# Root-mean-square roots on four columns of 128 tokens, spread over the rows by TensorE, in a two-layer trunk on one Trainium2 core

## The reference

```python
def rmsnorm(x, g, eps=1e-6):
    xf = x.astype(F32)
    y = xf * lax.rsqrt(jnp.mean(xf * xf, axis=-1, keepdims=True) + eps)
    return (y * g.astype(F32)).astype(x.dtype)

for i in range(DEPTH):
    h = rmsnorm(x, norm_mix[i])
    x = x + (even_mixer if i % 2 == 0 else mlstm_mixer)(h, ...)
    x = x + peer(rmsnorm(x, norm_ffn[i]), ...)
    gate = sigmoid(rmsnorm(x, norm_ple[i]) @ ple_gate[i])
    x = x + gate * (p[i] @ ple_w[i])
return rmsnorm(x, norm_final)
```

## Time and profile before

| | before |
|---|---|
| median of 3 runs | 4248.63 us (4247.73 to 4251.1) |
| the profiled execution | 4250.18 us, span 4248.7 us, mean granted clock 0.994 |
| TensorE busy | 4185.4 us, 99% |
| VectorE, ScalarE, POOL busy | 2731.2 us (64%), 2064.9 us (49%), 1319.8 us (31%) |
| chain that ended last | PE 83%, DVE 6%, ACT 5%, issue 4%, POOL 1% |

### The profile page before, as it was taken

One profiled execution on the slowest core, in us unless ns is written; L12 is line 12 of the kernel. 1 busy time (PEld: TensorE's weight loads), 2 busy tenths in 40 slices (PEclk: granted clock), 3 DMA queues, 4 the chain that ended last, 5 costly groups with the idle time before them and its releaser, 6 DMA issues.

```text
span 4248.7 us, 61062 instructions
## 1 busy us (share of the span) xinstructions
PE 4185.4 (99%) x19171; PEld 3421.3 (81%) x19171; DVE 2731.2 (64%) x5672; ACT 2064.9 (49%) x4042; POOL 1319.8 (31%) x1648
## 2 busy tenths in 40 slices
PE   8998999999999999999999999999999999999998
PEld 6666888888888888888788888888888888888886
DVE  3647898777764444444777765997778744444445
ACT  3756333877763333333555553335777833333334
POOL 0311446877750000001200002457778710000001
PEclk9999999999999999999999999999999999999999
DMA  3112334555566565652222223335555575655542
GB/s 116 60 58 77 110 117 158 206 188 186 184 248 233 173 217 173 205 185 99 84 86 84 89 84 105 111 134 195 185 205 181 203 275 176 214 176 202 188 138 85
DMA packets 181372, 657.75 MB, mean 155 GB/s; under 512 B 17664, under 2 KB 17792, under 8 KB 176352
## 3 DMA queue, kind: packets, MB, share of 16 engines
q1 hardware_dynamic: 102960, 371.41, 25.7%
q0 software_dynamic: 41392, 217.39, 14.5%
q10 hardware_dynamic: 36864, 67.13, 4.3%
HBM read 511.09 MB, written 144.77 MB: 154 GB/s over the span
## 4 chain that ended last, share of the span: by engine, by line
PE 83%; DVE 6%; ACT 5%; issue 4%; POOL 1%; ACTq 0%; DVEq 0%; POOLq 0%
PE ps L185 76%; PE ps L1564 2%; ACT first_scaled L1583 2%; ACT w_hi L158 1%; DVE od_tmp L371 1%; POOL w_lo L171 1%; DVE w_lo L164 1%; PE ps L1147 1%; PE ps L874 1%; PE ps L1837 1%; ACT gelu L1074 0%; PE ps L2063 0%; PE ps L522 0%; PE ps L523 0%; DVE gate_group L1493 0%
## 5 line engine op out<-in xcount | busy, mean ns | idle before, releaser
L164 DVE TENSOR_TENSOR w_lo<-w_raw,w_hi 128x1024 fp32r<-128x1024 f32 x585 | 719.4, 1230 | 1050.2 <-ACT w_hi L158 1046.4
L158 ACT ACTIVATE w_hi<-w_raw 128x1024 fp32r<-128x1024 f32 x694 | 734.6, 1058 | 1096.9 <-PE ps L185 961.1
L185 PE MATMUL ps<-h_hi,w_hi 128*128 128x512 f32 x3080 | 1214.4, 394 | 20.6 <-DVE h_lo L314 10.7
L185 PE MATMUL ps<-h_hi,w_lo 128*128 128x512 f32 x3080 | 1201.2, 390 | 0.0
L185 PE MATMUL ps<-h_lo,w_hi 128*128 128x512 f32 x3080 | 1200.5, 390 | 0.0
L185 PE MATMUL ps<-y_hi,w_hi 128*128 128x512 f32 x2368 | 926.6, 391 | 2.4 <-POOL w_lo L171 1.7
L185 PE MATMUL ps<-y_hi,w_lo 128*128 128x512 f32 x2368 | 923.3, 390 | 0.0
L185 PE MATMUL ps<-y_lo,w_hi 128*128 128x512 f32 x2368 | 923.0, 390 | 0.0
L1545 POOL TENSOR_SCALAR second_hot<-iota,token_keys 128x128 fp32r<-128x128 f32 x1024 | 724.9, 722 | 0.0
L185 PEld LDWEIGHTS ps<-h_hi,w_hi 128*128 128x128 f32 x3080 | 579.2, 188 | 152.1 <-issue 22.5
L185 PEld LDWEIGHTS ps<-h_hi,w_lo 128*128 128x128 f32 x3080 | 578.9, 188 | 122.6
(11 more groups left out here) (347 smaller groups left out, 3529.3 us busy)
## 6 DMA issues: line engine op xcount, KB each, us to landing
w_raw<-in_u SPq DMA_DIRECT2D x256, 512.0 KB, 3.3
w_raw<-in_v SPq DMA_DIRECT2D x256, 512.0 KB, 3.3
gates<-gate_group POOLq DMA_DIRECT2D x36, 2048.0 KB, 7.9
acts<-gelu ACTq DMA_DIRECT2D x256, 256.0 KB, 2.1
gate_block<-gates POOLq DMA_DIRECT2D x32, 2048.0 KB, 18.0
gelu_block<-acts POOLq DMA_DIRECT2D x30, 2048.0 KB, 11.5
w_raw<-in_od_in SPq DMA_DIRECT2D x65, 512.0 KB, 3.3
w_raw<-in_ev_in SPq DMA_DIRECT2D x33, 512.0 KB, 3.3
```

What stands on the lines that cost most here:

```text
L158: self.nc.scalar.activation(self.wh[:, slot % SPL, :], self.raw[:, slot, :], ACT.Copy).then_inc(self.sig("w_hi_ready").sem, 1)
L164: self.nc.vector.tensor_tensor(self.wl[:, slot % SPL, :], self.raw[:, slot, :], self.wh[:, slot % SPL, :].bitcast(F32), ALU.subtract).then ...
L185: ins = self.nc.tensor.matmul(out, a[:, s, w], b[:, k, :], start=first and j == 0 and m == 0, stop=last and j == n - 1 and m == 2)
```

## The change

A new class `Root` makes all eight roots. The sum over partitions is turned round: the squares are the weights, 128 tokens at a time, and one column of ones moves. Four such matmuls leave four columns, 128 tokens in the partitions of each. ScalarE and VectorE work on these 128x4. TensorE spreads them back over the rows: the column, broadcast to 128 columns, is the weights, and the identity moves. ScalarE copies the spread rows to SBUF (`act_keep`), except for the final norm, whose scalings read PSUM.

```diff
+class Root:
+    def pe_sums(self, pe, squares, part=0):
+        p = self.p
+        for j in range(TT):
+            c = part * TT + j
+            ins = p.nc.tensor.matmul(p.ps[:, self.bank, c:c + 1], squares[:, j * P:(j + 1) * P], p.ones[:, 0:1],
+                                     start=True, stop=True, skip_group_check=True)
+        return ins
+    def dve_parts(self, dve):
+        p = self.p
+        p.nc.vector.tensor_reduce(p.root[:, :], p.ps[:, self.bank, 0:TT * self.parts].rearrange(
+            "p (k j) -> p j k", j=TT), AX_X, ALU.add).then_inc(self.added.sem, 1)
+    def act_make(self, act):
+        a, p = self.p.nc.scalar, self.p
+        src = p.ps[:, self.bank, 0:TT]
+        if self.parts > 1:
+            act.wait_ge(self.added.sem, self.added.at(1))
+            src = p.root[:, :]
+        a.activation(p.root[:, :], src, ACT.Copy, scale=1.0 / (DK * P), bias=EPS).then_inc(self.made.sem, 1)
+        act.wait_ge(self.made.sem, self.made.at(1))
+        a.activation(p.root[:, :], p.root[:, :], ACT.Sqrt).then_inc(self.made.sem, 1)
+    def dve_invert(self, dve):
+        dve.wait_ge(self.made.sem, self.made.at(2))
+        self.p.nc.vector.reciprocal(self.p.root[:, :], self.p.root[:, :]).then_inc(self.inverted.sem, 1)
+    def pe_spread(self, pe):
+        p = self.p
+        pe.wait_ge(self.inverted.sem, self.inverted.at(1))
+        for j in range(TT):
+            ins = p.nc.tensor.matmul(p.ps[:, self.bank, j * P:(j + 1) * P], p.root[:, j:j + 1].to_broadcast([P, P]),
+                                     p.ident[:, :], start=True, stop=True, skip_group_check=True)
+        ins.then_inc(self.spread.sem, 1)
+    def pe_product(self, pe, u, out, rh, rl):
+        def tile(k):
+            if k == 3:
+                self.pe_spread(pe)
+        p = self.p
+        p.product(pe, u, u % RAW, out, rh, rl, wait_tile=tile).then_inc(p.sig("w_used").sem, 1)
+    def act_keep(self, act, rstd):
+        act.wait_ge(self.spread.sem, self.spread.at(1))
+        self.p.nc.scalar.activation(rstd, self.p.ps[:, self.bank, :], ACT.Copy).then_inc(self.kept.sem, 1)
```

`parts` is 8 in the front (a set of four columns for each tile), 2 in the final norm, 1 elsewhere. `Norm` calls these in place of L307, L309, L320, L326 and L341; the one-column table load stays. The spread is placed inside the next unit, ahead of its tile 3, by `pe_product`:

```diff
 EvenFront, TensorE
+            if n == 1:
+                self.norm.root.pe_product(pe, u0 + 1, p.ps[:, self.EARLY_BANK[1], :], p.hh, p.hl)
+                continue
 EvenFront, ScalarE
         for n in range(1, len(EARLY)):
             ahead(n)
+            if n == 1:
+                self.norm.root.act_keep(act, self.norm.rstd)
 EvenSSD, TensorE
-        t.matmul(p.ps[:, 3, :], p.ones[:, :], self.total, start=True, stop=True).then_inc(self.ss.sem, 1)
+        self.root.pe_sums(pe, self.total).then_inc(self.ss.sem, 1)
         pe.wait_ge(self.zl.sem, self.zl.at(DK))
-        for k in range(DK, 2 * DK):
+        pe.wait_ge(self.ov.sem, self.ov.at(DK - 1))
+        self.root.pe_product(pe, u0 + DK, p.ps[:, 6, :], p.hh, p.hl)
+        for k in range(DK + 1, 2 * DK):
 EvenSSD, VectorE
-        dve.wait_ge(self.root.sem, self.root.at(2))
+        self.root.dve_invert(dve)
         ahead(DK)
-        v.reciprocal(self.rstd, self.rstd).then_inc(self.rd.sem, 1)
-        dve.wait_ge(self.rd.sem, self.rd.at(1))
+        self.root.dve_wait(dve)
 TopK, TensorE and ScalarE
-        for n in range(1, L):
+        self.norm.root.pe_product(pe, u0 + 1, p.ps[:, 5, :], self.norm.hi, self.norm.lo)
+        for n in range(2, L):
...
         split(2)
+        self.norm.root.act_keep(act, self.norm.rstd)
 Ple, TensorE
             for q in range(4):
+                if 4 * j + q == 6:
+                    self.norm.root.pe_spread(pe)
...
         if self.final:
             self.last.pe_total(pe)
+            self.last.root.pe_spread(pe)
 Ple, ScalarE: act_keep after take(3); VectorE
         split(2)
         self.norm.dve_root(dve)
         split(3)
+        self.norm.root.dve_wait(dve)
...
-                                       in1=self.last.rstd, op0=ALU.mult, op1=ALU.mult).then_inc(self.fin.sem, 1)
+                                       in1=p.ps[:, self.last.bank, :], op0=ALU.mult, op1=ALU.mult
+                                       ).then_inc(self.fin.sem, 1)
```

```diff
 OddMixer, ScalarE
         split(0, 0)
+        self.norm.root.act_keep(act, self.norm.rstd)
+        split(0, 1)
         act.wait_ge(self.gin.sem, self.gin.at(1))
         a.activation(r["e1"], r["ab"], ACT.Exp, scale=-1.0).then_inc(self.gact.sem, 1)
         act.wait_ge(self.gin.sem, self.gin.at(2))
         a.activation(r["ln"], r["ab"], ACT.Ln).then_inc(self.gact.sem, 1)
-        split(0, 1)
 OddMixer, VectorE
-        def conv(n, j):
+        def take(n, j):
             dve.wait_ge(used.sem, n * 4 + h0 + j + 1)
             v.tensor_tensor(qk[:, j, CONV - 1:], p.ps[:, j, :], rstd, ALU.mult).then_inc(self.taken.sem, 1)
+        def conv(n, j):
...
+        take(0, 0)
         conv(0, 0)
+        take(0, 1)
         link(v.reciprocal(r["rc"], r["ab"]))
```

More of the change, by code:

```diff
@@ L274, in start, with __init__, dve_wait @@
     ld.base += 16
+class Root:
+    def __init__(self, p, bank, parts=1):
+        self.p, self.bank, self.parts = p, bank, parts
+        counts = (("root_cols_made", 2), ("root_inverted", 1), ("root_spread", 1), ("root_kept", 1),
+                  ("root_parts_added", 1 if parts > 1 else 0))
+        self.made, self.inverted, self.spread, self.kept, self.added = (Mark(p.sig(n), k) for n, k in counts)
+    def pe_sums(self, pe, squares, part=0):
[37 more added lines that the diff above has]
+        self.p.nc.scalar.activation(rstd, self.p.ps[:, self.bank, :], ACT.Copy).then_inc(self.kept.sem, 1)
+    def dve_wait(self, dve):
+        dve.wait_ge(self.kept.sem, self.kept.at(1))
@@ L283, in __init__ @@
         counts = (("norm_hi", DK if pair else 0), ("norm_lo", DK if pair else 0), ("squared", DK),
-                  ("sumsq", DK), ("root", 2), ("norm_rstd", 1), ("squares_added", self.summed - 1 if total is not None else 0))
-        self.nh, self.nl, self.sq, self.ss, self.ro, self.rd, self.sa = (Mark(p.sig(n), k) for n, k in counts)
+                  ("sumsq", DK), ("squares_added", self.summed - 1 if total is not None else 0))
+        self.nh, self.nl, self.sq, self.ss, self.sa = (Mark(p.sig(n), k) for n, k in counts)
+        self.root = Root(p, bank, DK if total is None else 1 + alone)
         if scratch:
@@ L318, in dve_root @@
     def dve_root(self, dve):
[L319 to L321 removed]
+        if self.root.parts > 1:
+            dve.wait_ge(self.ss.sem, self.ss.at(DK))
+            self.root.dve_parts(dve)
+        self.root.dve_invert(dve)
     def pe_sum(self, pe, k):
@@ L325, in pe_sum @@
         pe.wait_ge(self.sq.sem, self.sq.at(k + 1))
-        p.nc.tensor.matmul(p.ps[:, self.bank, :], p.ones[:, :], self.s2[:, k % 2, :], start=k == 0, stop=k == DK - 1
-                           ).then_inc(self.ss.sem, 1)
+        self.root.pe_sums(pe, self.s2[:, k % 2, :], k).then_inc(self.ss.sem, 1)
     def pool_sums(self, pool):
@@ L2074, in tensor @@
         for j in range(4):
-            if j < 2:
+            if j == 0:
+                self.norm.root.pe_product(pe, h0, p.ps[:, 0, :], p.hh, p.hl)
+            elif j == 1:
                 p.product(pe, h0 + j, (h0 + j) % RAW, p.ps[:, j, :], p.hh, p.hl).then_inc(used.sem, 1)
@@ L2332, in body @@
             lo(n, 0)
+            take(n, 0)
             conv(n, 0)
@@ L2340, in body @@
             lo(n, 2)
+            take(n, 1)
             conv(n, 1)
```

30 lines of the change are left out of this document (13 added, 17 removed).

## The result

The changed kernel takes 4275.86 us (median of 4 runs, 4275.16 to 4279.19) against 4248.85 of the kernel before, run beside it: ratio 1.0064, 95% interval 1.0052 to 1.0076. It is 27.0 us slower, where 7.1 were forecast, and outside the range given. The two profiled spans are 4273.9 and 4248.7 us, 25.2 apart; what follows divides those 25.2.

The account below looks back on a forecast made before the run. TensorE, busy 4185 of 4248.7 us, was taken as the bound. Terms 0.9 + 1.2 + 1.4 + 4.8 + 0.3 - 1.5 = +7.1 us gave 4255.7 against the median 4248.63; range 4250.0 to 4263.7.

Parts of the forecast that it names:

- The front: Even mixer's first norm: sums +1.1, a spread of 0.9 against a wait of 1.11 gone, -0.2; together +0.9 us.
- the first three run at half clock: Front: of eight sums, three at half clock add some 0.25 us each, the five others 0.07 each: +1.1.
- 0.25 each: Front: extra us for each of three small sums at half clock, twice 0.93 against the old sum's 1.71.
- Rival 1: Clock falls where TensorE waits or runs small matmuls: +8.0 us, 4263.7, slower; chance 0.22.
- four places: Where the clock might fall: the front's sums (3.5 us), each Ple wait (1.4), the odd mixer's long wait (1.7).
- The odd mixer: Exp late, VectorE's chain 2.3 us late, 1.97 back from the convolution, TensorE's waits gone without gain: +0.3 us.
- Rival 2: Odd mixer gives back its waits of 1.71 and 1.96 and 1.7 of half clock: 4250.0 us; chance 0.14.
- SSD: The SSD's norm: TensorE waits 0.2 us, spread 0.9, sum's 0.07, no old wait to recover: +1.2 us.
- Ple: Each of two stages: TensorE waits 1.3 us ahead of the seventh embedding group, spread 0.9, sum and restart: +2.4 us.
- the second TopK: Second TopK stage, with an old wait of 0.72 us in the same place: up to +0.7 us.
- the last norm: Kernel's end: short reciprocal on few columns, less the spread and scalings from PSUM: -1.5 us.
- The first TopK: First TopK stage: the spread delays unit 1, so scaled rows and TensorE's next start come later: +0.7 us.

Follow-up runs that it names:

- f2: The changed kernel with the spread of both Ple norms behind the eighth embedding group instead of ahead of the seventh: 4272.83 us.
- e4: The kernel before with four unused one-column ScalarE instructions ahead of the gates' loop: 4254.95 us.
- f4: The kernel before with the last norm alone by columns and five unused ScalarE instructions ahead of the gates' loop: 4245.74 us.
- g0: The kernel before with the last norm by columns and five unused ScalarE instructions, run again as a reference: 4246.49 us.
- g2: The f4 kernel with the take of the second convolution's input ahead of the reciprocal, nothing else: 4246.76 us.

## Why the prediction was wrong

**The front (+0.9, measured 8.8).** The step that failed is "the first three run at half clock, ... the five others 0.07 each". It took the moment at which the clock rises from the old trace, as if it were given by time. It is given by what TensorE does, and the change replaced, at just that place, one 512-column matmul by four of one column. All eight sums ran at half clock, and the eight product tiles and the first of unit 1 with them. The term "0.25 each" for the sums at half clock was wrong too: its own prices, twice 0.93 against 1.71, give 0.15, and the traces show none (2.98 us a tile, 2.99 before). Rival 1 had the place and the sign, but a price of 3.5, from rows behind the 16-column matmuls, for one stretch. Of its four places two had the fall, the front and the odd mixer's long wait; unit h0 had one that it did not name, and neither Ple wait brought one.

**The gates (not in the sum, measured 5.2).** No step of the working looked at a stage without an edit. The change is four ScalarE instructions longer ahead of a loop whose entry lay five instructions from a fetch. The old trace had the sign of it, a high half 2.9 us behind the branch, with "<-issue", and a wait of 0.14 to 0.18 behind it on TensorE, so no slack at all.

**The odd mixer (+0.3, measured 3.5).** The chain was right: Exp late, 1.97 given back by the convolution, no gain from TensorE's waits, one long wait for the gate rows. The failed term is the clock, twice: unit h0 and the spread, taken at 2.2 and 0.9, which at half clock ended 1.7 later than forecast and carried the gate rows with them (1.8 late), and 1.8 behind the wait of 5.2. In f2, the same code without the fall in h0, Exp is 2.7 late, where 2.5 was forecast, the gate rows 0.2, and the stage lost 1.2. With the old code up to 1.7 comes and goes as well (e4, f4, g0). Rival 2 fell: g2 has TensorE's wait gone and the time unchanged.

**Odd output and second gates (0, measured 1.3 and 0.9)**: the 16 bytes. Not thought of.

**Right in size**: SSD 1.2 (1.0), Ple 2.4 twice (2.5, 2.4), the second TopK 0.7 (0.8), the last norm -1.5 (-1.9, varying from -1.1 to -2.0), a spread at 0.8 to 0.9 and the column operations at 0.17 to 0.20. The first TopK lost 1.2 for 0.7, 0.3 of it by the addresses. The Ple stage is the clearest: f2 splits its 2.4 into a wait of 1.4 that another place for four matmuls avoids, and 1.0 that stays.

## What to carry to other kernels

A root made on few columns saves VectorE's time, which is worth nothing where TensorE is the bound, and costs TensorE a spread; it pays where nothing else is left to do, at the last norm (1.1 to 2.0 us here). Before trusting a sum over edits, ask of each edit whether it changes what TensorE does around the point where its clock rises, and of the whole diff which loops' entries and which tiles' addresses it moves. A stage without an edit that changes its time is to be looked at first, not last: at its turns, and at the distance between equal matmuls.

## What the runs showed of the hardware that was not expected

- More matmuls can take less time: eight 512-column sums added to the front shortened it by 3.0 us, since the granted clock was full from 16.0 us instead of 37.2.
- A turn of ScalarE's loop over the gates (476 instructions) costs 2.7 to 3.0 us before its first instruction in all fifteen traces. A second gap of 1.8 to 2.3 us follows behind the first, second or fifth instruction, or nowhere near, by where the loop's entry stands; it cost TensorE some 2 us a turn where it came ahead of the third. One unused instruction was worth 6.9 us in one kernel and 7.7 in another; four cost the stage 4.7 in a third.
- Product matmuls of the same shape start 0.227 us apart, and in one stage 0.2334 on the average, depending on where their tiles lie: with a new tile of 16 bytes the starts of all products spread by 4.1 us over the kernel, of which 2.5 show in the times of four stages. Which operand has to lie where was not tried.
- The stretches of half clock differ between executions of the same code in place: a stage came out -2.2 to 0.8 us different inside the even mixer, 0 to 1.7 in the odd one with the old code and 1.2 to 3.5 with the new. One execution can't price a fall of the clock.
